# The attention stage of a 512-token network on one core: eight head steps written out and woven, masks as a product, staging copies dropped

## The reference, cut to what matters

```python
z = einsum('bqhd,bkhd->bhqk', q_blk, k) * scale
causal = k_pos[None, :] < (start + arange(Q_BLOCK))[:, None]
log_keep = where(causal, log_sigmoid(-z), 0.0)
later = cumsum(log_keep, axis=3, reverse=True) - log_keep
log_w = where(causal, log_sigmoid(z) + later, -inf)
out = einsum('bhqk,bkhd->bqhd', exp(log_w), v)
```

## Time and profile before

| what | us |
|---|---|
| median of three runs (2969.61 to 2979.86) | 2972.72 |
| the profiled execution, its own time | 2968.51 |
| its span, first to last instruction | 2966.7 |
| TensorE busy | 2617.2 (88%), mean granted clock 0.924 |
| VectorE / ScalarE / GpSimd busy | 1015.2 / 1031.3 / 1311.9 |

### The profile page before, as it was taken

How to read it: one execution, slowest core, us unless ns; L and a number is a source line. 1 busy time by engine, 2 the same in 40 slices (tenths; PEclk the granted TensorE clock), 3 DMA queues, 4 the chain that set the end, 5 groups by cost and what they waited for, 6 DMA issues and landing times. The chain is left out here.

```text
span 2966.7 us, 31775 instructions
## 1 busy us (share of the span) xinstructions
PE 2617.2 (88%) x11088; PEld 2065.9 (70%) x11088; DVE 1015.2 (34%) x1515; ACT 1031.3 (35%) x1428; POOL 1311.9 (44%) x770
## 2 busy tenths in 40 slices
PE   7999999666799999999999899559999999687887
PEld 5888878433488888888887576228888877565655
DVE  2223120123252221422213521544322339513973
ACT  4333322444443333432332323334333334223442
POOL 4555444200155554555544343114655545255843
PEclk9999989877899999999998999678999989898897
DMA  3224322100023233222232122002323323221111
GB/s 119 96 95 135 106 99 94 41 0 0 18 75 99 95 97 105 79 98 99 92 106 77 58 85 64 0 0 71 111 94 99 102 76 107 70 78 57 58 63 57
DMA packets 69178, 228.16 MB, mean 77 GB/s; under 512 B 8787, under 2 KB 13139, under 8 KB 68988
## 3 DMA queue, kind: packets, MB, share of 16 engines
q1 hardware_dynamic: 63456, 218.63, 22.4%
q10 hardware_dynamic: 4812, 5.55, 0.7%
q0 software_dynamic: 848, 3.15, 0.3%
HBM read 222.68 MB, written 6.84 MB: 77 GB/s over the span
## 5 line engine op out<-in xcount | busy, mean ns | idle before, releaser
L369 POOL TENSOR_TENSOR wl_sb<-raw_sb,wh_sb 128x1024 fp32r<-128x1024 f32 x401 | 969.8, 2421 | 965.2 <-ACT wh_sb L361 961.5
L1548 PE MATMUL banks<-xh_sb,wh_sb 128*128 128x512 f32 x2064 | 816.1, 395 | 91.0 <-POOL wl_sb L369 64.5
L1549 PE MATMUL banks<-xh_sb,wl_sb 128*128 128x512 f32 x2064 | 812.1, 393 | 0.0
L1550 PE MATMUL banks<-xl_sb,wh_sb 128*128 128x512 f32 x2064 | 810.9, 393 | 0.0
L361 ACT ACTIVATE wh_sb<-raw_sb 128x1024 fp32r<-128x1024 f32 x401 | 423.8, 1059 | 800.6 <-DMA raw_sb<-weights 796.8
L1548 PEld LDWEIGHTS banks<-xh_sb,wh_sb 128*128 128x128 f32 x2064 | 392.9, 190 | 183.2 <-issue 68.9
L1550 PEld LDWEIGHTS banks<-xl_sb,wh_sb 128*128 128x128 f32 x2064 | 393.0, 190 | 83.0
L1549 PEld LDWEIGHTS banks<-xh_sb,wl_sb 128*128 128x128 f32 x2064 | 393.0, 190 | 81.1
L1548 PE MATMUL banks<-hh_sb,wh_sb 128*128 128x512 f32 x704 | 273.9, 389 | 0.0
L1549 PE MATMUL banks<-hh_sb,wl_sb 128*128 128x512 f32 x704 | 273.9, 389 | 0.0
L1550 PE MATMUL banks<-hl_sb,wh_sb 128*128 128x512 f32 x704 | 273.9, 389 | 0.0
(11 more groups left out here) (380 smaller groups left out, 2793.7 us busy)
## 6 DMA issues: line engine op xcount, KB each, us to landing
raw_sb<-weights SPq DMA_DIRECT2D x404, 512.0 KB, 3.4
scratch<-scratch ACTq DMA_DIRECT2D x1, 2560.0 KB, 12.1
x_sb<-x_in SPq DMA_DIRECT2D x8, 256.0 KB, 8.6
mix_sb<-scratch POOLq DMA_DIRECT2D x1, 2048.0 KB, 9.0
out<-hf_sb SPq DMA_DIRECT2D x8, 256.0 KB, 2.2
turn<-mix_sb SPq DMA_DIRECT2D x4, 256.0 KB, 4.6
mix_sb<-turn SPq DMA_DIRECT2D x4, 256.0 KB, 4.5
turn<-mix_sb ACTq DMA_DIRECT2D x4, 256.0 KB, 2.5
```

What stands on the lines that cost most here:

```text
L369: pool.tensor_tensor(wl[:, slot, :], raw[:, slot, :], wh_f[:, slot, :], ALU.subtract).then_inc(w_split, 1)
L1548: pe.matmul(dst, wh[:, q, cols], in_hi, start=first, stop=False)
L1549: pe.matmul(dst, wl[:, q, cols], in_hi, start=False, stop=False)
L1550: return pe.matmul(dst, wh[:, q, cols], in_lo, start=False, stop=last)
```

## The change

The hardware loop becomes eight steps written out, u = 0 to 8, where iteration u issues the head of step u together with the tail of step u - 1. The causal mask is added on TensorE, as one more product for each diagonal tile: the identity times a 128x128 table `later_mask` (0 above the diagonal, -1e30 elsewhere), which is loaded once at the start by one more DMA on ScalarE's queue (64 KB). Both sets of `affine_select` go, and with them GpSimd's part in the stage. The six staging copies of each pass go; products read `qkT`, `va`, `vd` in place. |z|, exp, log, the VectorE sum, the suffix sums and the weights are done in two parts (tiles 1 to 3 first, tile 0 second), each part with its own signal. A row block is turned back with one ScalarE copy in place of qb + 1, into one buffer `pT` of 4x512 in place of two. The credits go, as the first steps skip the waits.

```diff
-                        for kb in range(4):
-                            d = buf[:, OFF[kb]:OFF[kb] + P]
-                            last = pool.affine_select(out=d, in_=d, pattern=[[1, P]], compare_op=ALU.is_gt,
-                                                      fill=0.0, base=0, channel_multiplier=-1)
-                        last.then_inc(done, 1)
...
+            def logits(u, tiles):
+                if u == 0:
+                    pe.wait_ge(tiles_freed, FREE0 + TILE["attn.v"] + 8)
+                    pe.wait_ge(mask_loaded, 16)
+                else:
+                    pe.wait_ge(a_w, 2 * u - (1 if tiles[0] else 0))
+                for kb in tiles:
+                    pe.matmul(zcols(kb), k_of(u)[:, P * kb:P * (kb + 1)], q_of(u)[:, P * kb:T], start=(kb != 3),
+                              stop=False, skip_group_check=True)
+                for kb in tiles:
+                    last = pe.matmul(zcols(kb)[:, 0:P], ident, later_mask, start=False, stop=False,
+                                     skip_group_check=True)
+                last.then_inc(a_z, 1)
...
+            for u in range(UNITS + 1):
+                old, new = u > 0, u < UNITS
+                if new:
+                    logits(u, (1, 2, 3))
+                if old:
+                    turn(u - 1, 2)
+                if new:
+                    logits(u, (0,))
+                if old:
+                    values(u - 1)
+                    turn(u - 1, 3)
+                if new:
+                    scores(u, 0)
+                    scores(u, 1)
+                if old:
+                    dilated_values(u - 1)
+                if new:
+                    suffix_sums(u, (1, 2, 3))
+                    suffix_sums(u, (0,))
+                    turn(u, 0)
+                    scores(u, 2)
+                    turn(u, 1)
+                    scores(u, 3)
...
+            def copy_turned(u, qb):
+                act.wait_ge(a_t, 4 * u + qb + 1)
+                if u:
+                    act.wait_ge(a_odl, u)
+                act.activation(pT[:, 0:qb + 1, P * qb:P * (qb + 1)],
+                               banks[:, 5, 0:P * (qb + 1)].rearrange("p (a n) -> p a n", n=P),
+                               ACT.Copy).then_inc(a_tc, 1)
...
+            for u in range(UNITS + 1):
+                old, new = u > 0, u < UNITS
+                if old:
+                    copy_turned(u - 1, 2)
+                if new:
+                    soften(u)
+                if old:
+                    copy_turned(u - 1, 3)
+                if new:
+                    logs(u)
+                if old:
+                    if u % 2 == 0:
+                        high_of(a_osb, 6, u // 2 - 1)
+                if new:
+                    exps(u, 0)
+                    exps(u, 1)
+                    weights_of(u, 1)
+                    weights_of(u, 0)
+                    copy_turned(u, 0)
+                    exps(u, 2)
+                    copy_turned(u, 1)
+                    exps(u, 3)
+                if old and u % 2 == 0:
+                    high_of(a_odl, 7, u // 2 - 1)
...
-                dve.tensor_copy(qp, at(qkT, i))
-                dve.tensor_copy(kp, at(qkT, i + 4))
-                dve.tensor_copy(qdp, at(qkT, i + 8))
-                dve.tensor_copy(kdp, at(qkT, i + 12)).then_inc(a_staged, 1)
...
+            for u in range(UNITS + 1):
+                new, paired = u < UNITS, u > 0 and u % 2 == 0
+                if new:
+                    spare_sum(u, 1)
+                    add_bias(u, 0)
+                    spare_sum(u, 0)
+                    add_bias(u, 1)
+                if paired:
+                    low_of(a_oev, 6, u // 2 - 1, u - 1)
+                if new:
+                    normalise(u, 0)
+                    normalise(u, 1)
+                    add_bias(u, 2)
+                    normalise(u, 2)
+                    add_bias(u, 3)
+                    normalise(u, 3)
+                if paired:
+                    low_of(a_oev2, 7, u // 2 - 1, u)
...
+            act.dma_start(gain[:, 0:P], consts[:, NCONST:NCONST + P]).then_inc(mask_loaded, 16)
```

More of the change, by code:

```diff
@@ L539, in build @@
         sp_ = ab
[L540 to L541 removed]
+        pT = chunks(region(16384, 4 * T))
+        ssb = [hf_f[:, T * j:T * (j + 1)] for j in range(2)]
+        later_mask = gain[:, 0:P]
         Z01 = banks[:, 0, :]
@@ L584, in attention_tensor @@
-        def attention_tensor(pe):
[L585 to L631, removed]
-                    for kb in range(4):
-                        last = pe.matmul(banks[rows, 6, P * kb:T], vp[:, P * kb + 64 * e:P * kb + 64 * e + 64],
-                                         packed(wk[e], kb), start=(kb == 0), stop=(kb == 3),
-                                         skip_group_check=True)
-                    last.then_inc(a_osb, 1)
-                    turn(3)
-                    pe.wait_ge(a_tc, 4 * u + 5)
-                    if e == 0:
-                        pe.wait_ge(a_oev2, i + 1)
-                    for kb in range(4):
-                        last = pe.matmul(banks[rows, 7, P * kb:T], vdp[:, P * kb + 64 * e:P * kb + 64 * e + 64],
-                                         packed(pT[e], kb), start=(kb == 0), stop=(kb == 3),
-                                         skip_group_check=True)
-                    last.then_inc(a_odl, 1)
-            pe.wait_ge(a_oev, 5)
-            pe.wait_ge(a_oev2, 5)
@@ new lines, in attention_vector, with spare_sum, add_bias, normalise @@
+        def attention_vector(dve):
+            def spare_sum(u, part):
+                dve.wait_ge(a_ln, 2 * u + 2 - part)
+                buf = two(sp_[u % 2])[part]
+                dve.scalar_tensor_tensor(buf, Z23 if part else Z01, 0.0, buf, ALU.max, ALU.add).then_inc(a_spr, 1)
+            def add_bias(u, qb):
+                n = P * (qb + 1)
+                dve.wait_ge(a_s, 4 * u + qb + 1)
+                if 4 * u + qb >= 2:
+                    dve.wait_ge(a_t, 4 * u + qb - 1)
+                dve.tensor_tensor(ssb[qb % 2][:, 0:n], banks[:, 3 + qb % 2, 0:n], strip[:, u, T - n:T],
+                                  ALU.add).then_inc(a_sadd, 1)
+                dve.wait_ge(a_sadd, 4 * u + qb + 1)
+                dve.tensor_reduce(small[:, NMX + qb:NMX + qb + 1], ssb[qb % 2][:, 0:n], AX.X, ALU.max,
+                                  negate=True).then_inc(a_mx, 1)
+            def normalise(u, qb):
+                n = P * (qb + 1)
+                dve.wait_ge(a_exp, 4 * u + qb + 1)
+                dve.reciprocal(small[:, RL + qb:RL + qb + 1], small[:, LSUM + qb:LSUM + qb + 1]).then_inc(a_rl, 1)
+                dve.wait_ge(a_rl, 4 * u + qb + 1)
+                dve.tensor_scalar(ssb[qb % 2][:, 0:n], ssb[qb % 2][:, 0:n], small[:, RL + qb:RL + qb + 1], None,
+                                  ALU.mult).then_inc(a_p, 1)
+            def low_of(done, bank, pair, n):
+                dve.wait_ge(a_oh, n)
+                c = pair + 4 * (bank - 6)
+                dve.tensor_tensor(xl[:, c, :], banks[:, bank, :], xh_f[:, c, :], ALU.subtract).then_inc(done, 1)
+            dve.wait_ge(strip_in, 16)
+            for u in range(UNITS + 1):
[16 more added lines that the diff above has]
+                    low_of(a_oev2, 7, u // 2 - 1, u)
```

172 lines of the change are left out of this document (76 added, 96 removed).

## The result

| | before | after |
|---|---|---|
| median, us | 2976.29 | 2867.84 (2866.52 to 2871.31) |
| ratio, 95% interval | | 0.9638 [0.9625, 0.9651] |
| profiled execution, its own time (span) | 2968.51 (2966.7) | 2871.31 (2869.2) |
| the stage, end of the last v product to the first output product | 249.9 | 151.5 |

One run of before, 4507.14, was disturbed; it stands in the median 2976.29 and not in the ratio, and the other three have 2972.72, 104.9 us above the changed kernel. The changed kernel was timed twice more beside the one before: 0.9666 [0.9646, 0.9687] (2875.84 against 2974.43, 98.6 us) and 0.9660 [0.9638, 0.9681] (2870.76 against 2973.58, 102.8 us).

What follows compares the result with a forecast made beforehand. No engine is full in the attention stage; a chain paces it at 30.7 us a step. Steps of 16.7 save 98.5 us: 2968.5 - 98.5 = 2870.0, median 4.2 above, so 2874 us; range 2864 to 2893.

Steps and rivals of the forecast that it cites:

- (e): Rival, attention stage: no slow stretch behind the first suffix sums, steps at TensorE's 15.2 to 16; 2864 to 2868 us, chance 0.10.
- The chain: Attention step, suffix sums to next suffix sums: instructions behind each other sum to 16.75 us, where a step was 30.7.
- the 1.1 us for ends: Whole attention stage: 1.1 us added for ends of clock stretches and the pair copies in odd steps.
- The head: Stage start to first suffix sums: TensorE begins at 549.15, then 11.1 us with logits at 1.2 GHz, to 560.3.
- The tail: Last suffix sums to next stage's first product: today's order, 19.8 us less 2.0 for the clock, 17.8, to 697.4.
- TensorE at 15.2 a step: TensorE's own work in a new attention step, 15.2 us at 2.4 GHz, 1.5 below the chain.
- (a): Rival: the clock falls once a step around turns 0 and 1, 16 to 24 us back, 2890 to 2898; chance 0.12.
- (b): Rival: ScalarE's strict order makes each head wait for the old tail; about 23 us a step, 2911; chance 0.03.
- (c): Rival: clock stays at 1.2 GHz for the whole stage, TensorE's 30.4 us binds, about 2972, no change; chance 0.015.
- (d): Rival: fetching written-out step bodies on three engines stalls each step; at four waits, 13.6 us, 2983; chance 0.015.
- (f): Rival: each ScalarE function set change costs double its load, 10 to 21 us back, 2884 to 2895; chance 0.02.
- Periods that alternate: Sign that the forecast is wrong: attention step periods that alternate or exceed 18 us.

Runs made afterwards that it cites:

- the two filled kernels: Unused products put in TensorE's wait: six a step in the kernel before, 2956.52 us (0.9933); four in the changed kernel with its weave removed, 2923.48 us (0.9832).
- the kernel with early scores: Changed kernel reordered: scores 2 before the suffix sums, turn 0 between their parts, biases of row blocks 0 and 1 and turn 0's copy earlier; 2863.47 us, 0.9624.
- the one that issues it later: The kernel with early scores, plus two unused products in TensorE's first wait and the mask table's DMA after the first inputs are scaled; 2855.74 us, 0.9609.
- the written-out kernel: The kernel before with the four passes of its attention loop written out on all engines, nothing else; 2965.16 us, ratio 0.9970.

## Why the prediction was right, point by point

**The size.** Forecast were 98.5 us saved in the stage, 2870.0 for the profiled execution and 2874 for the median; measured 98.4, 2871.31 and 2867.84. Three comparisons of medians gave 105 (without the disturbed run), 99 and 103 us. The step at fault for the 6 us between 2874 and 2867.84 is the last one, which carried over that before's median stood 4.2 above its profiled execution; the changed kernel's stood 3.5 below. The time of one execution scatters by 10 us and more with the clock in other stages. By that scatter 2867.84 lies just outside the forecast's own band of 2868 to 2883 and at the edge of (e); the steps in the stage say that it is the forecast's mechanism.

**The chain.** 16.75 a step was forecast, 17.1 is the mean of what was measured. Of its terms: suffix sums to turn 0, 4.44 for 4.3 (596.74 to 601.18); turn 0 to scores 2, 0.20 as said; the split |z|, exp and log as said. The 0.35 is `high_of` in every second step, 0.37 there, which stood in the 1.1 us for ends, and 0.14 in the suffix sums.

**The head.** First logits 549.62, 2.1 behind the last v product, for 549.15 plus nothing: the stretch before ended 0.4 later in this execution, and the hand-over costs 0.05. To the first suffix sums 10.5 for 11.1, and that is luck, since two terms of the sum were wrong and cancel. It left out a load of exp's function set, which in the new order only the first step has and which the kernel before had hidden in its wait (549.17):

```profile
553.56 0.60 ACT L661 ACTIVATE mix_sb<-banks 128x512 f32<-128x512 f32 x1 [0.66 <-PE banks L582]
554.18 1.28 ACT L665 ACT_TABLE_LOAD   x1
555.47 1.36 ACT L665 ACTIVATE mix_sb<-mix_sb 128x768 f32<-128x768 f32 x2
```

And it put the logits with their masks at 6.0 us, at 1.2 GHz; here they ran at 2.4 and took 3.8. In the second profiled execution of the same kernel the clock stood at 1.2 GHz from 551 on, they took 5.8, and the first suffix sums came 12.4 us behind the first logits.

The first period, 19.7, is 2.8 above the 16.9 of such a step, for the 2.0 forecast. All of it is the suffix sums at 1.2 GHz, 7.23 us to turn 0 (560.11 to 567.34) for 4.44; the second step's logits were at 2.4 GHz again. The tail, 682.43 to 698.96, is 16.5 for 17.8, mostly by the same term: suffix sums and turn 0 went from 7.39 to 4.64, 2.75 less where the sum took 2.0, though its own 7.39 and 4.5 make it 2.9. So the price of one slow stretch was put 0.8 too low at both ends, once for the forecast and once against it.

The errors: start +0.5, head -0.6, first period +1.0, six periods +2.1 with 1.1 set aside for them, tail -1.3. That they come to 0.5 (698.96 for 698.5) is in part luck; that none is above 2.1 of 150 us is not.

**The clock** held: 1.00 from the second period to the end of the last. "Up to 46 us" of the saving was the clock by the sum of records; the two filled kernels show at least 14.5 and 24.3.

**TensorE at 15.2 a step** was rightly the lesser bound, but 0.7 short: in the kernel with early scores its records leave no gap and a step takes 15.9. The mask products are 0.3 of the difference, 1.2 us a step (604.13 to 604.92 and 606.45 to 606.87) for 0.9.

**The cost of writing out** was put at nothing by the row of the v products. The run shows no cost but 5.3 us less in the stage of before, 4.1 of them in TensorE's records, for a cause that stays open. The forecast did not suffer, as the new stage was built up from its own terms and not from the old stage's length.

**The mask load** on ScalarE's queue: ScalarE's first work, behind the first vector load, began at 4.61 us in place of 4.06, but at 4.11 in the kernel with early scores, which issues the mask load at the same place, and at 4.50 in the one that issues it later. So no cost of the load shows.

**The rivals.** (a), a fall of the clock once a step, did not happen. (b) falls with the periods; its own terms give 22.3 us a step and 2906, not 23 and 2911. (c) falls with the clock, (d) with the written-out kernel. (e)'s stage was not reached by this kernel, but its step of 15.2 to 16 was, by order alone. (f): a load begins at 610.85 and log at 612.14, that is 1.28 and 0.01 between. The Trainium skill (ScalarE: Activation LUTs, What ACT_TABLE_LOAD costs) adds about 1.38 us of drain to a switch; this trace does not agree, with 0.01 behind the load and 0.02 between the end of the copy at 592.94 and the load at 593.56.

"Periods that alternate" was named as a sign of being wrong. They alternate by 0.37 us, for a reason that was in the sum; the sign was badly chosen.

## What to carry to other kernels

Where no engine is full and one in-order engine stands in a fixed wait each step, ask what work of the neighbouring step could stand in that place: here taking the weave out gave back 73 of the 98 us, and a fill that changed nothing but the clock won 24 of those again. The Trainium skill says that whether TensorE stays warm is determined by the loop nest (TensorE: Matmul & The Clock Gate, Loop structure matters more than you think), and a clock of 0.97 woven against 0.80 unwoven, for the same products, agrees. Then add the chain and the engine's own work of one new step: whichever is longer is the period, and if it is the chain, move single instructions until it is not (16.9 and 17.3 to 15.9, where TensorE's records leave no gap). Judge such a change by the profile of its stage where other stages make the total scatter.

## What the runs showed of the hardware

More work on TensorE made the stage shorter in two kernels, by 14.5 and 24.3 us: six unused products of 512 columns in each step's wait raised the clock from 0.77 to 0.88, four raised it from 0.80 to 0.96. Two such products in one wait did not keep it up: they ran at 2.4 GHz (554.28 to 556.20), and the clock fell in the 2.9 us without work behind the next scores.

One binary can lose the clock at different instructions: the granted clock over 551.00 to 553.20, in the first logits, was 1.00 in one execution of the changed kernel and 0.50 in another, which made the stage 151.5 and 153.7 us.

The scatter of whole runs, 2963.6 to 2981.9 for the kernel before, lies in stages that work in bursts, and the same binary can differ by 8 us there. A stretch without clock changes repeats to 0.01 us: the three profiles of the changed kernel have steady periods of 16.91 to 16.92 and 17.28 to 17.29.
